# Low splits behind the keys' turn of block attention, made by GpSimd in place of VectorE

## What is computed

```python
q, k, v = (to_heads(t) for t in jnp.split(x @ w_qkv, 3, axis=-1))     # 16 heads of 64
q, k = partial_rotary(q, pos), partial_rotary(k, pos)
...
l_own = jnp.einsum('bhqd,bhkd->bhqk', qc, k_own) * scale
l_own = jnp.where(opos[None, :] <= cpos[:, None], l_own, NEG)
p = jax.nn.softmax(jnp.concatenate([l_sel, l_own], axis=-1), axis=-1)
o = p_sel @ vg + p_own @ v_own
return from_heads(o) @ w_o
```

## Time and profile before

| | |
|---|---|
| median of 3 runs | 2586.59 us (2586.37 to 2586.68) |
| the profiled execution | 2586.56 us, span 2584.5 us |
| TensorE busy in the span | 2559.7 us (99%), clock granted in full |
| VectorE, ScalarE, GpSimd busy | 1676.4, 1397.7, 61.2 us |
| `L211`, low splits on VectorE | 416, mean 2296 ns |
| `L204`, high splits on ScalarE | 425, mean 1914 ns |
| `L232`, low splits on GpSimd | 9, median 4609 ns |
| block attention, roughly | 1308 to 1429 us |

### The profile page before, as it was taken

How to read it: one execution, slowest core, us unless ns; L and a number is a source line. 1 busy time by engine, 2 the same in 40 slices (tenths; PEclk the granted TensorE clock), 3 DMA queues, 4 the chain that set the end, 5 groups by cost and what they waited for, 6 DMA issues and landing times.

```text
span 2584.5 us, 38075 instructions
## 1 busy us (share of the span) xinstructions
PE 2559.7 (99%) x14838; PEld 2224.3 (86%) x14838; DVE 1676.4 (65%) x1828; ACT 1397.7 (54%) x1665; POOL 61.2 (2%) x30
## 2 busy tenths in 40 slices
PE   8999999999999999999999999999999999999998
PEld 7888898888888988888888888888888888898887
DVE  7866687656766566666666666666766666665765
ACT  6744576446545664454466544545664454465544
POOL 0000000001000000000000000000000000000000
PEclk9999999999999999999999999999999999999999
DMA  7455534554555345555543555555345555543551
GB/s 275 147 201 189 183 141 178 194 195 175 197 193 179 134 156 185 193 179 195 190 154 129 180 194 181 194 185 180 124 169 183 192 179 195 184 159 114 194 195 65
DMA packets 63783, 454.35 MB, mean 176 GB/s; under 512 B 7120, under 2 KB 7376, under 8 KB 9280
## 3 DMA queue, kind: packets, MB, share of 16 engines
q1 hardware_dynamic: 62496, 449.67, 48.5%
q0 software_dynamic: 896, 3.05, 0.3%
q10 hardware_dynamic: 288, 0.15, 0.0%
HBM read 451.79 MB, written 1.05 MB: 175 GB/s over the span
## 4 chain that ended last, share of the span: by engine, by line
PE 93%; DVE 4%; ACT 2%; issue 1%; DMA 0%; SPq 0%; DVEq 0%; ACTq 0%
PE tb L500 28%; PE tb L505 15%; PE acc L289 10%; PE acc L290 10%; PE acc L291 10%; PE acc L255 2%; PE acc L257 2%; PE acc L258 2%; PE acc L500 1%; DVE w_lo L211 1%; PE tb L322 1%; PE acc L910 1%; PE acc L912 1%; PE acc L911 1%; PE acc L1010 1%; PE acc L505 1%
## 5 line engine op out<-in xcount | busy, mean ns | idle before, releaser
L211 DVE TENSOR_TENSOR w_lo<-raw,w_hi 128x2048 fp32r<-128x2048 f32 x416 | 953.8, 2296 | 293.0 <-ACT w_hi L204 292.3
L204 ACT ACTIVATE w_hi<-raw 128x2048 fp32r<-128x2048 f32 x425 | 813.0, 1914 | 311.5 <-PE acc L291 275.4
L500 PE MATMUL tb<-xT,w_hi 128*128 128x512 f32 x3168 | 792.1, 392 | 0.0
L500 PEld LDWEIGHTS tb<-xT,w_hi 128*128 128x128 f32 x3168 | 576.4, 188 | 108.5 <-DVE big L695 0.2
L505 PEld LDWEIGHTS tb<-xT,w_lo 128*128 128x128 f32 x3168 | 432.1, 190 | 31.0
L505 PE MATMUL tb<-xT,w_lo 128*128 128x256 f32 x3168 | 441.7, 282 | 0.0
L289 PE MATMUL acc<-w_hi,cat 128*128 128x512 f32 x1024 | 402.6, 393 | 0.0
L290 PE MATMUL acc<-w_hi,cat 128*128 128x512 f32 x1024 | 399.8, 390 | 0.0
L291 PE MATMUL acc<-w_lo,cat 128*128 128x512 f32 x1024 | 398.7, 389 | 0.0
L291 PEld LDWEIGHTS acc<-w_lo,cat 128*128 128x128 f32 x1024 | 192.2, 188 | 41.1
L289 PEld LDWEIGHTS acc<-w_hi,cat 128*128 128x128 f32 x1024 | 192.7, 188 | 38.8 <-DVE cat L706 2.7
(11 more groups left out here) (347 smaller groups left out, 2883.2 us busy)
## 6 DMA issues: line engine op xcount, KB each, us to landing
raw<-in_stream SPq DMA_DIRECT2D x425, 1024.0 KB, 4.8
h<-in_x SPq DMA_DIRECT2D x4, 256.0 KB, 5.0
raw<-in_stream SPq DMA_DIRECT2D x2, 512.0 KB, 6.3
xn<-in_gates POOLq DMA_DIRECT2D x2, 512.0 KB, 7.8
gain<-in_gains POOLq DMA_DIRECT2D x2, 512.0 KB, 5.2
out<-xn SPq DMA_DIRECT2D x2, 512.0 KB, 2.8
cst<-in_consts SPq DMA_DIRECT2D x1, 832.0 KB, 11.3
big<-in_pT POOLq DMA_DIRECT2D x2, 256.0 KB, 5.5
```

The lines of the kernel that those rows point to most:

```text
L204: act.activation(w_hi[:, k % SPLIT, :], raw[:, k % RAW, :], ACT.Copy).then_inc(hi_done, 1)
L211: dve.tensor_tensor(w_lo[:, k % SPLIT, :], raw[:, k % RAW, :], w_hi[:, k % SPLIT, :], ALU.subtract).then_inc(lo_done, 1)
L500: return pe.matmul(bank, w_hi[:, c % SPLIT, at:at + P], xT[:, kt, :, :].rearrange("p a t -> p (a t)"), start=first, stop=last)
```

## The change

Three low splits of block attention, those at the end of the products of keys 4, 7 and 10 (chunks c+7, c+10 and c+13), go from VectorE to GpSimd. VectorE goes from the keys' turn straight on to the reciprocals and probabilities. At the end of the products of values 5, 8 and 11 it waits until GpSimd's split is counted, so that the splits stay in order; the next split is VectorE's again.

```diff
                     if kind == "moba" and unit[1] % 3 == 1:
                         turn_dve(dve, i, c, unit[1])
-                    if not (kind == "moba" and unit[1] == FED - 1):
+                    if kind == "moba" and unit[1] % 3 == 2:
+                        dve.wait_ge(lo_done, c + unit[1] + SPLIT)
+                    if not (kind == "moba" and (unit[1] == FED - 1 or unit[1] % 3 == 1)):
                         split_lo(dve, c, unit[1] + SPLIT)
...
                         pool.dma_start(gain[:, :], gains[0, :].partition_broadcast(P)).then_inc(*sig("gain_in", BRIDGE, 16))
+                if kind == "moba":
+                    for e in range(4, FED, 3):
+                        pool_lo(pool, c + e + SPLIT)
                 if kind == "mla":
```

## The result

| | before | after |
|---|---|---|
| median | 2586.63 us (2586.37 to 2586.69, 6 runs) | 2596.26 us (2595.93 to 2597.79, 6 runs) |
| ratio | | 1.0038, interval 1.0027 to 1.0048 |
| profiled execution, its span | 2586.56, 2584.5 us | 2596.18, 2594.1 us |

The change makes the kernel slower by 9.6 us, 0.37%. The forecast was slower by 6.0 us, with a range up to 7.2: the sign and the main mechanism were right, the size was not.

What follows compares the result with a forecast made beforehand. The prediction took TensorE's own work plus its few waits to bound the kernel. Delays of +2.11, +2.04 and +1.86 us at pairs 1, 3 and 5, in all +6.0 on 2586.6, gave 2592.6 us, range 2589.4 to 2593.8.

Steps and rivals of the forecast that it cites:

- What bounds the kernel: TensorE, busy 2559.7 of 2584.5 us; other engines count only through its waits, here for probabilities in block attention.
- the prize of 3 us: TensorE's waits at pairs 1 and 5, about 1.46 + 1.37 us and crumbs: 3 us or 0.12% to gain at most.
- The hold: At pairs 1, 3 and 5 GpSimd's split stops VectorE's two-SBUF-input multiplication L1250 until 0.14 us before the split ends.
- a small spread table counts as a full input: Reciprocals spread from a small table count as L1250's and L1251's second SBUF input; taken from the skill page's wording only.
- Who comes first: At pair 1 GpSimd starts at 1349.33, L1250 could near 1349.5; GpSimd wins by about 0.15 us, likewise at pairs 3, 5.
- The waits of TensorE: L1193's waits for the probabilities of pairs 1, 3 and 5 become near 3.6, 2.1 and 3.3 us.
- The sum with the hold: Delays of the probabilities at pairs 1, 3 and 5, +2.11, +2.04 and +1.86 us, in all +6.0 us.
- Granted clock: TensorE's clock stays at full speed in block attention despite waits of 3.6 in place of 1.5 us; costed at nothing.
- No hold: Rival, chance 0.13: multiplications run freely, but VectorE waits for GpSimd's split, delaying scores by +3.2 us: 2589.8 us.
- VectorE first: Rival, chance 0.06: L1250 and L1251 precede and hold GpSimd's split, 1.0 us three times, +6.2 us in all: 2592.8 us.
- the stalls simply go: Rival, chance 0.04: nothing is held, VectorE's wait for GpSimd meets spare time, TensorE's waits vanish: 2583.6 us.

Runs made afterwards that it cites:

- e5_late: Kernel before, all splits on VectorE, those of products 4, 7, 10 and 11 moved later, the last two into VectorE's idle time: 2584.27 us against 2587.08.
- e6_gp_late: e1_one_input with VectorE's splits of products 5, 8 and 11 moved between maxima and probabilities of pairs 2, 4 and 7: 2583.38 us against 2587.08 before.
- e1_one_input: Changed kernel with block attention's reciprocals written to PSUM, so the scaling multiplications have one SBUF input: 2590.09 us against 2586.79 before.
- e2_fill: Changed kernel with 58, 32 and 56 unused matmuls ahead of TensorE's waits for the probabilities of pairs 1, 3 and 5: 2593.44 us against 2586.79 before.
- e7_after_again: The changed kernel itself, run once more: 2595.78 us against 2587.08 before, ratio 1.0034.
- e9_writes: e5_late plus three idle GpSimd memsets of 2048 columns at each of the change's three places: 2584.04 us against 2587.15 for the kernel before.
- e3_gp_after: Changed kernel, but GpSimd starts each split only when VectorE has finished that pair's probabilities: 2594.47 us against 2586.79 before.
- e8_reads: e5_late plus an idle GpSimd tensor_tensor of 2048 columns on unused memory at the change's three places: 2596.03 us against 2587.15 for the kernel before.

## Why the prediction came out as it did

- **What bounds the kernel:** right. All the new waiting lies at pairs 1, 3 and 5, as named, and the prize of 3 us was right too: e5_late and e6_gp_late collect 3.0 and 3.4 us of it.
- **The hold:** right in all its parts. L1250 was forecast at 4.6 us ending 0.1 us before GpSimd does (its own work starts 0.13 us before GpSimd's end, and its end lies 0.29 us behind it: there the wording was loose). That a small spread table counts as a full input, the one link without a row, was shown by e1_one_input. Who comes first was decided by 0.15 us as worked out: GpSimd at 1350.22, L1252 at 1350.37.
- **The waits of TensorE:** forecast 3.6, 2.1 and 3.3 us, measured 3.48, 1.99 and 3.39.
- **The sum with the hold:** +6.0; with the clock kept up (e2_fill) +6.05.
- **The step that failed** is "Granted clock: ... waits of 3.6 us in place of 1.5 don't give me a reason for a change". This term was put at zero and measured 2.7 us (after against e2_fill, by the stretch) to 3.9 us (e7_after_again against it). Behind its start the trace of before holds no wait over 1.5 us, so it could not say whether waits of 3.6 us would bring a fall; such a term has to be bounded, not dropped. After's rows at the lower level give its size: from 1357.7 to 1360.3 us matmuls of 256 columns stood 0.21 us apart in place of 0.12, so each microsecond at 1.2 GHz lost 0.44. By the averages of the windows each of the two stretches had 3.4 us at that level, which makes 3.0 us in all. The price alone could have been read before: at the very start of its trace, behind a wait of 2.39 us, matmuls of the same 256 columns stand 0.21 us apart until 11.5 us and 0.12 apart from 13.2 us on, though the granted clock is given as 1.00 in both stretches, so that it is not shown there what slowed them.

```profile
9.15 0.42 PE L257 MATMUL tb<-xT,w_hi 128*128 128x256 f32 x1
9.37 0.41 PE L258 MATMUL tb<-xT,w_lo 128*128 128x256 f32 x1
...
13.20 0.28 PE L257 MATMUL tb<-xT,w_hi 128*128 128x256 f32 x1
13.32 0.28 PE L258 MATMUL tb<-xT,w_lo 128*128 128x256 f32 x1
```

- **What the range lacked besides:** up to 1 us from the start of the kernel, which moves between executions more than the first runs showed: on another chip the kernel before took 2585.81 to 2587.97 us in 26 runs. And in the profile of e7_after_again the clock's fall cost 1.2 us more than in the first one of the same code.
- **The rivals:** "No hold" was priced at +3.2, and e1_one_input measured +3.3 (+3.37 by the stretch), through the very waits named; that its fall of the clock hardly showed in the time was luck for a sum without one. "VectorE first" was 6.2 against 6.96: each split came 1.3 us later, not 1.0. That the stalls simply go is out for this code, since GpSimd's end is later than VectorE's next split; it becomes true (e6_gp_late) once that split is moved.

## What to carry to other kernels

Before work goes from VectorE to GpSimd, look at what VectorE makes in those microseconds: its instructions with two inputs in SBUF stood still here until GpSimd's split was all but over, so the move freed nothing. It paid only with the reciprocals in PSUM and VectorE's next split moved away (e6_gp_late), and then hardly more than a better order on VectorE alone (e5_late). If such an order is wanted, try the same order on the engine that had the work, and look for idle time of that engine behind a wait (here 1.8 to 2.3 us ahead of the reciprocals of pairs 2, 4, 6 and 7). And where an edit can lengthen TensorE's waits (here from 1.5 to 3.4 us), price the matmuls behind them at the lower clock too, at least as one end of the range.

## What the runs showed of the hardware

- A VectorE tensor_tensor with two SBUF inputs stands still while a GpSimd instruction that reads SBUF, and began before it, runs: 0.42 us became 4.67, with its second input only a table of four numbers a partition. Its work began 0.12 to 0.14 us before the recorded end of GpSimd's instruction. With one of the two inputs in PSUM it took 0.42. The Trainium skill (SBUF — State Buffer, section Who interferes with whom) states this rule, and these runs agree. It also says that such an instruction does not contend with a GpSimd instruction that only writes: e9_writes agrees (0.43 us beside the memsets).
- A tensor_scalar of four elements a partition, with its input and output in SBUF, is stopped as well, and by a GpSimd instruction that only writes too: for 0.17 us it took 1.53 and 1.42 in e6_gp_late, beside a split, and 1.31 in e9_writes, beside a memset. The trace of before has one of two elements a partition, L1666 at 1822.74 us, that took 0.90 us and ended within 0.03 us of GpSimd's second copy of the earlier trace rows.
- GpSimd's tensor_tensor of 2048 columns took 4.6 us with two regions as inputs, 3.60 with the same region twice, and its memset of 2048 columns 1.81 (three in 5.55).
- TensorE's granted clock fell to 0.50 behind single waits of 3.4 to 3.5 us (after, e7_after_again), of 3.3 us (e3_gp_after, e8_reads) and of 2.54 us (e8_reads). It stayed full behind single waits of 1.99 us (after), 2.15 us (e1_one_input) and 2.30 us (e3_gp_after). The fall came at the earliest within the wait and at the latest 1.4 us behind it. In e1_one_input it averaged 0.57 from 1406 to 1408 us, behind its second wait for scores, of 2.0 us, which stood 7.6 us behind one of 2.1 us: so it can also fall behind a wait of 2 us. What makes the difference was not tried.
